# Attention loops with one softmax: products with the values ahead of the turns of the next pair

## What is computed

```python
s = jnp.einsum('bqhd,bkhd->bhqk', qb, k).astype(jnp.float32) * scale
s = jnp.where(key_pos[None, :] <= q_pos[:, None], s, -jnp.inf)
p = jax.nn.softmax(s, axis=-1)
return jnp.einsum('bhqk,bkhd->bqhd', p.astype(v.dtype), v)
```

## Time and profile before

| | |
|---|---|
| median of three runs | 4166.4 us (4159.61 to 4171.67) |
| the profiled execution | 4176.12 us, span 4173.6 us |
| TensorE (PE) busy | 3923.3 us, 94% |
| weight loads (PEld) busy | 3330.1 us, 80% |
| VectorE (DVE), ScalarE (ACT), GpSimd (POOL) busy | 1654.7, 1443.4, 1400.4 us |
| mean granted clock of TensorE | 0.967 |

### The profile page before, as it was taken

One profiled execution on the slowest core, in us unless ns is written; L12 is line 12 of the kernel. 1 busy time (PEld: TensorE's weight loads), 2 busy tenths in 40 slices (PEclk: granted clock), 3 DMA queues, 4 the chain that ended last, 5 costly groups with the idle time before them and its releaser, 6 DMA issues. The chain is left out here.

```text
span 4173.6 us, 56453 instructions
## 1 busy us (share of the span) xinstructions
PE 3923.3 (94%) x23092; PEld 3330.1 (80%) x23092; DVE 1654.7 (40%) x3386; ACT 1443.4 (35%) x2330; POOL 1400.4 (34%) x517
## 2 busy tenths in 40 slices
PE   6998999999989899999989999999999898889999
PEld 5777877887877788788869988888888787767887
DVE  5735142322383523332261454311114676764111
ACT  3435243342234433333332364211122444433221
POOL 2211323343321123244322321223222567653442
PEclk8899999999998999999999999999999999989999
DMA  3221414334222132334411210122212111103332
GB/s 115 56 83 39 136 57 136 113 124 131 75 56 78 44 119 74 113 113 152 126 51 61 83 24 23 52 61 68 68 51 67 42 51 41 41 21 91 86 102 75
DMA packets 476076, 323.12 MB, mean 77 GB/s; under 512 B 31449, under 2 KB 472236, under 8 KB 475820
## 3 DMA queue, kind: packets, MB, share of 16 engines
q1 hardware_dynamic: 422112, 268.18, 22.3%
q10 hardware_dynamic: 53708, 51.33, 3.6%
HBM read 315.74 MB, written 2.16 MB: 76 GB/s over the span
## 5 line engine op out<-in xcount | busy, mean ns | idle before, releaser
L96 POOL TENSOR_TENSOR w_lo<-w_raw,w_hi 128x2048 fp32r<-128x2048 f32 (+6 forms) x329 | 1158.0, 3524 | 2499.3 <-ACT w_hi L228 2498.9
L228 ACT ACTIVATE w_hi<-w_raw 128x2048 fp32r<-128x2048 f32 (+3 forms) x278 | 471.8, 1698 | 1094.8 <-PE psum L264 1066.3
L262 PE MATMUL psum<-xF_hi,w_hi 128*128 128x512 f32 x1232 | 494.6, 401 | 20.4 <-ACT a_relud L1579 7.1
L264 PE MATMUL psum<-xF_hi,w_lo 128*128 128x512 f32 x1232 | 486.9, 395 | 0.0
L263 PE MATMUL psum<-xF_lo,w_hi 128*128 128x512 f32 x1232 | 484.9, 394 | 0.0
L262 PE MATMUL psum<-ffn_h_hi,w_hi 128*128 128x512 f32 (+1 forms) x1056 | 375.8, 356 | 2.2 <-issue 1.3
L263 PE MATMUL psum<-ffn_h_lo,w_hi 128*128 128x512 f32 (+1 forms) x1056 | 374.0, 354 | 0.0
L264 PE MATMUL psum<-ffn_h_hi,w_lo 128*128 128x512 f32 (+1 forms) x1056 | 373.9, 354 | 0.0
L262 PEld LDWEIGHTS psum<-xF_hi,w_hi 128*128 128x128 f32 x1232 | 233.3, 189 | 77.0 <-ACT a_relud L1579 8.7
L264 PEld LDWEIGHTS psum<-xF_hi,w_lo 128*128 128x128 f32 x1232 | 233.2, 189 | 52.8
L263 PEld LDWEIGHTS psum<-xF_lo,w_hi 128*128 128x128 f32 x1232 | 233.6, 190 | 49.9
(11 more groups left out here) (543 smaller groups left out, 8291.4 us busy)
## 6 DMA issues: line engine op xcount, KB each, us to landing
w_raw<-in_w_in_dram SPq DMA_DIRECT2D x56, 1024.0 KB, 5.3
ada_w<-in_ada_w_dram ACTq DMA_DIRECT2D x48, 1024.0 KB, 6.9
w_raw<-in_ffn_w_in_dram SPq DMA_DIRECT2D x88, 512.0 KB, 5.1
w_raw<-in_w_in_dram SPq DMA_DIRECT2D x78, 512.0 KB, 4.2
w_raw<-in_ffn_w_out_dram SPq DMA_DIRECT2D x32, 704.0 KB, 4.4
w_raw<-in_w_branch_dram SPq DMA_DIRECT2D x74, 256.0 KB, 4.6
w_raw<-in_hg_w_in_dram SPq DMA_DIRECT2D x32, 512.0 KB, 4.6
w_raw<-in_na_w_qkv_dram SPq DMA_DIRECT2D x12, 1024.0 KB, 5.1
```

The lines of the kernel that those rows point to most:

```text
L96: return eng.tensor_tensor(pair.lo, src, pair.hi.bitcast(F32), ALU.subtract)
L228: act.activation(self.w(j).hi, self.raw_w(j), ACT.Copy).then_inc(*self.high_done.up(1))
L262: pe.matmul(out, left.hi, right.hi, start=first, stop=False)
L264: return pe.matmul(out, left.lo, right.hi, start=False, stop=last)
```

## The change

TensorE issues the products of pair `s-2` ahead of the turns of pair `s-1`. The waits in front of each, the buffers, and the lists of the other engines stay as they are.

```diff
                 for s in range(NU // 2 + 2):
                     if s < NU // 2:
                         scores(s)
+                    sums(s - 2)
                     turn(s - 1)
-                    sums(s - 2)
```

## The result

After the change the kernel takes 4189.0 us (median of 4 runs, 4184.5 to 4194.6), against 4167.2 of the kernel before beside it: a ratio of 1.0055, 95% interval [1.0034, 1.0076]. It is slower by over 0.3%, outside the range of 4158 to 4182, and the forecast of "no change" is wrong. The profiled execution of after took 4194.6 us (span 4192.8), that of before 4176.1 (span 4173.6).

What follows compares the result with a forecast made beforehand. TensorE, busy 3923 of 4173.6 us, was taken to bound the kernel. Stall 0, cover 0, last pair +3.0 and seams 0 sum to +3.0 us: 4169.4 us, 0.07% more, within a range of 4158 to 4182.

Steps and rivals of the forecast that it cites:

- Clock and seams: Rival: shifted clock rise in sparse and latent stages, up to 3.3 us, plus seams' 7, either way: 4159 to 4180; chance 0.16.
- The repeated stall: TensorE's eight NA waits of 0.56 us for ScalarE's copy stay unchanged: 0, bounds -4.2 to +4.2 us.
- the stall is filled: Rival: products run while turns wait in NA, sparse and memory stages, 6.4 us gained less 3.0: 4163; chance 0.10.
- The cover of the copies inside the loop: One scores group between turns and their products still hides ScalarE's copies: 0, with 0.17 us left at the tightest place.
- the cover is too short: Rival: products wait for late copies in each of 114 inner steps, 34 us in all: 4200; chance 0.08.
- Hidden slack: Rival: NA's modelled matmul times hide up to 28.8 us of waits, giving 4140 at most; chance 0.03.
- The last pair: At each stage's end the last products wait for their copy, 0.44 or 0.43 us: +3.0 us, bounds 0 and 6.7.
- The seams: Group-to-group transitions on TensorE in 80 pairs with 64-row scores cost the same in sum: 0, bounds -7 to +7 us.

Runs made afterwards that it cites:

- c4: Kernel before, with the new order only in the last two steps of each of the seven stages: 4177.7 us, ratio 1.0016.
- c2: Changed kernel plus three unread matmuls in the start wait of the sparse and NA stages: 4164.3 us, ratio 0.9991 to the kernel before.
- d1: Kernel before (old order) plus three unread matmuls in the start wait of the sparse and NA stages: 4158.4 us, ratio 0.9981.
- a1: The changed kernel run once more, new order in all seven stages, against the kernel before: 4188.0 us, ratio 1.0041.
- a3: Kernel before, with the new order in the two sparse stages alone: 4180.8 us, ratio 1.0026.
- c1: Kernel before (old order) plus one unread one-column matmul per pair between turns and products in the sparse stages: 4193.9 us, ratio 1.0071.
- b1: Kernel before, with the new order only in steps 0 to 7 of the sparse stages: 4172.1 us, ratio 1.0016.
- b2: Kernel before, with the new order only from step 8 on in the sparse stages: 4175.2 us, ratio 1.0017.
- b4: Kernel before, with the new order and widest-to-narrowest tiles in the sparse stages: 4162.8 us, ratio 0.9990.
- d2: Changed kernel plus four unread 128 x 128 matmuls before each pair's products in the sparse stages: 4193.8 us, ratio 1.0076 to the kernel before.
- e1: Kernel before (old order) plus two start matmuls in sparse stages, widest tiles first in latent and differential stages: 4142.4 us, ratio 0.9935.
- a2: Kernel before, with the new order in the neighbourhood stage (NA) alone: 4174.7 us, ratio 1.0018.
- a4: Kernel before, with the new order in the two latent and two memory stages alone: 4167.7 us, ratio 0.9993.

## Why the prediction was wrong, step by step

The step that failed is the clock. The sum, 0 + 0 + 3.0 + 0, has no term for it; it stands only in the rival "Clock and seams", at 3.3 us at most. The runs put 15 to 17 of the 23 us there. The terms in their order:

- *The repeated stall: 0.* Right, with a misread row: the eight waits were seven of 0.56 and one of 0.26. The seven are there after the change, 0.52 for 0.56, ended by the same copy, and the one at the start is gone: 0.6 us less in all. ScalarE's order releases both orders at the same event, and the rival "the stall is filled" is dead.
- *The cover of the copies inside the loop: 0.* Right, at the tight place too. With that the rival "the cover is too short" fell. "Hidden slack", which wanted a faster kernel, fell too, since the time rose.
- *The last pair: +3.0.* The mechanism was right, with 0.34 for 0.44 (sparse) and 0.35 for 0.43 (NA). What the step missed is the pair before it: no scores stand between its turns and its products either. In sparse and memory it takes the place of an old wait, as written; in NA and, by the waits of after, in the latent stages it is new. By these rows the ends cost 3 x 0.70 + 4 x 0.35 = 3.5 us; c4, made to measure this alone, did not settle it.
- *The seams: 0.* Mis-sized. I compared modelled ends. In the new order the overlaps come out as expected (0.06 to 0.07 around the scores, 0.17 between products and turns: 2419.71 + 2.00 against 2421.54), but the groups' modelled lengths changed with their neighbours, the turn's from 1.09 to 1.04 and the products' from 1.90 to 2.00. Only start to start counts: 0.05 a step, in 80 steps 4 us, inside the bounds of ±7 and off the value taken. With the ends and the shorter stall that makes 6.9, and c2 minus d1 measured 7.0 ± 1.5 or 4.7 ± 2.8. The Trainium skill (TensorEngine Tiling, Key Properties) says that changing the tiling mode drains TensorE; as many changes before as after would have made the sum 0. By these rows it is not: the turns take 0.98 in front of scores on 64 rows and 0.93 in front of products, while the products take 1.82 or 1.83 in front of either.
- *Clock and seams, "up to 3.3 us either way".* This is the step that failed, and two thirds to three quarters of the loss; the chance given to passing the bound this way was 0.03. I priced the clock from two layers' rows of the same code, 2.0 and 1.3 us, which showed how a draw scatters and not what an emptier step does. And I let it go either way, where the edits that emptied the sparse steps lowered the clock (a1, a3, c1, and b1 by 6.8 ± 2.6 us at the lower level; b2 and b4 are within the noise) and the ones that filled steps or the start wait raised it (c2, d1, d2, e1). What was to be read in the earlier trace rows is how much lay at the lower level at all: 2 x (1 - 0.74) x 55.85 = 29 us in the first sparse stage, 25 in the second, with steps between that level and the next.

What the runs show of the mechanism: a sparse stage begins at the lower level, and the narrow first pairs leave it there for some pairs. In the profiles with the old order in that loop (before, a2, a4, c4) the clock rose behind the fifth to tenth of the sixteen turns, in those with the new order (after, a1, a3) behind the eighth to tenth. In b1 it was the eighth and ninth, in b2, whose steps are new from the ninth on, the sixth and eleventh. With one seam more it was the tenth both times, with four matmuls more the second and third, with the start filled by three matmuls (c2, d1) ahead of the first. The old and the new order overlap here (c4, with the old order in all but its last steps, has 34.1 us twice, as after has), which is why the table's means, not single profiles, carry the argument. Not shown is that the 0.1 us per step (3.91 against 3.80) is the whole of the new order's effect on the clock: c1's seam empties a step by 0.8 us and keeps the clock down little longer than the new order's 0.1 does (41.0 us twice, against 34.1 to 41.0). NA's falls were not taken apart; with the start filled there was none in the new order (one profile, c2).

## What to carry to other kernels

Before you price a reordering on TensorE, list the stages that begin at the lower level and how long they stay there: here an edit worth 0.1 us a step went with 29 us more at that level, and that is priced from the whole of that time, not from its scatter. In these runs such a stage gained from starting with its widest tiles, or with a few throw-away matmuls in a wait that is there anyway, and lost by the reordering. Price seams from start to start of the very sequence that the change makes, or run that sequence once; and where a loop's last steps lack a part, count every step that lacks it.

## What the runs showed of the hardware

- TensorE stayed at the lower level while it had work without a gap: 17 us busy of 17 at 0.50 (a1's sparse stage), and some 37 us in NA. In a1 and a2 the fall in NA came behind a wait of 2.71 us for the exp, in after earlier, within the stage's first scores (2.73 us long in place of 2.00), behind a wait of 2.45 us for a DMA; the earlier trace rows has a wait of 2.72 with no fall behind it.
- The Trainium skill (TensorE: Matmul & The Clock Gate, Part 1) says that the throttled state is the default, that activity releases it, and that the ramp's penalty is under 1% of a typical kernel span, so that one should not fit to a specific count of cold matmuls. The first agrees with the sparse stages, which begin at 0.50. The second agrees in part: in the sparse stages the clock rose while TensorE worked, but not within the 17 us of a1 that were busy throughout. The third does not hold here, if it is taken for all the time at the lower level: before has 270 us of it, worth 116 to 135 by the slope or by half (an estimate), about 3% of 4168; the difference between the orders, 15 to 17 us, is 0.4%.
- A matmul of one column on 64 rows between two groups on 128 rows cost 0.8 us at the lower level, for two instructions (4.61 against 3.80).
- Four matmuls of 128 x 128 in fp32 took 1.00 us at the full level and 1.87 at the lower.
